# All sixteen modulation tiles of the even output projection moved into the opening stage, six per pair of weight tiles

## The reference, cut to what matters

```python
def adaln(cvec, w, b):
    mod = jax.nn.silu(cvec) @ w + b
    return jnp.split(mod, 6, axis=-1)          # shift1 scale1 gate1 shift2 scale2 gate2
...
    hs = modulate(rmsnorm(xs, norm1_g[l]), m_lat[0], m_lat[1])
...
    # layer 0: even_project, diff_attention, multiscale_pool, even_output (ends in "@ w_out")
    xs = xs + m_lat[2] * out_s
    hs = modulate(rmsnorm(xs, norm2_g[l]), m_lat[3], m_lat[4])
    xs = xs + m_lat[5] * swiglu(hs, w_ffn_in[l], w_ffn_out[l])
```

## Time and profile before

| | |
|---|---|
| median of 3 runs | 2965.31 us |
| the profiled execution, its own time | 2965.08 us |
| its span in the trace | 2962.3 us |
| PE busy | 2772.4 us (94%) |
| PE weight loads busy | 2646.7 us (89%) |
| DVE busy | 1310.1 us (44%) |
| ACT busy | 817.0 us (28%) |
| POOL busy | 765.0 us (26%) |
| `wmt` tiles of 512 KB by L191 | 56, 3.5 us from issue to landing |

### The profile page before, as it was taken

One profiled execution on the slowest core, in us unless ns is written; L12 is line 12 of the kernel. 1 busy time (PEld: TensorE's weight loads), 2 busy tenths in 40 slices (PEclk: granted clock), 3 DMA queues, 4 the chain that ended last, 5 costly groups with the idle time before them and its releaser, 6 DMA issues. The chain is left out here.

```text
span 2962.3 us, 40371 instructions
## 1 busy us (share of the span) xinstructions
PE 2772.4 (94%) x16562; PEld 2646.7 (89%) x16562; DVE 1310.1 (44%) x2125; ACT 817.0 (28%) x1277; POOL 765.0 (26%) x338
## 2 busy tenths in 40 slices
PE   5998888999999999999899996879999999999997
PEld 4997767989999999999899994549999999999996
DVE  5688985953222222222654444544422222222225
ACT  4214665251111111111532222542511111111113
POOL 1562223531111111111322212334321111111112
PEclk9998999999999999999999997999999999999999
DMA  6433102411111111110234434305111111111101
GB/s 241 165 130 87 22 15 107 157 58 43 43 42 42 42 42 42 42 42 18 108 121 148 150 113 187 111 24 217 43 58 43 42 42 42 42 38 38 40 13 64
DMA packets 57724, 227.13 MB, mean 77 GB/s; under 512 B 7376, under 2 KB 17296, under 8 KB 47120
## 3 DMA queue, kind: packets, MB, share of 16 engines
q1 hardware_dynamic: 56032, 225.12, 21.5%
q10 hardware_dynamic: 1584, 0.51, 0.1%
HBM read 191.52 MB, written 29.88 MB: 75 GB/s over the span
## 5 line engine op out<-in xcount | busy, mean ns | idle before, releaser
L220 PE MATMUL ps<-hh,wi_hi 128*128 128x384 f32 x2112 | 707.9, 335 | 0.0
L221 PE MATMUL ps<-hl,wi_hi 128*128 128x384 f32 x2112 | 705.8, 334 | 0.0
L222 PE MATMUL ps<-hh,wi_lo 128*128 128x384 f32 x2112 | 705.7, 334 | 0.0
L1166 DVE TENSOR_TENSOR hid<-ps,hid 128x384 f32<-128x384 f32 x132 | 73.6, 557 | 989.3 <-ACT hid L871 989.3
L220 PEld LDWEIGHTS ps<-hh,wi_hi 128*128 128x128 f32 x2112 | 396.7, 188 | 1.0 <-issue 0.3
L221 PEld LDWEIGHTS ps<-hl,wi_hi 128*128 128x128 f32 x2112 | 396.7, 188 | 1.0 <-issue 0.3
L222 PEld LDWEIGHTS ps<-hh,wi_lo 128*128 128x128 f32 x2112 | 396.7, 188 | 0.0
L871 ACT ACTIVATE hid<-ps 128x384 f32<-128x384 f32 x132 | 64.9, 492 | 1127.9 <-PE ps L222 1127.9
L998 POOL TENSOR_TENSOR wi_lo<-raw_in,wi_hi 128x2048 fp32r<-128x2048 f32 x44 | 202.9, 4611 | 645.4 <-ACT wi_hi L861 645.3
L1177 DVE SCALAR_TENSOR_TENSOR x<-ps,mod,x 128x128 f32<-128x128 f32 (+1 forms) x704 | 326.9, 512 | 77.0 <-PE ps L222 72.9
L220 PE MATMUL ps<-hid_hi,wo_hi 128*128 128x384 f32 x1056 | 354.0, 335 | 2.8 <-DVE x L1177 2.7
(11 more groups left out here) (268 smaller groups left out, 4542.9 us busy)
## 6 DMA issues: line engine op xcount, KB each, us to landing
raw_in<-in_w_ffn_in_dram SPq DMA_DIRECT2D x44, 1024.0 KB, 4.7
wmt<-in_w_mod_t_dram SPq DMA_DIRECT2D x56, 512.0 KB, 3.5
raw_out<-in_w_ffn_out_dram SPq DMA_DIRECT2D x22, 1024.0 KB, 4.7
gla_spill<-turn SPq DMA_DIRECT2D x24, 576.0 KB, 2.8
oraw<-in_w_in_odd_dram SPq DMA_DIRECT2D x24, 512.0 KB, 4.5
wmt_odd<-in_w_mod_t_dram SPq DMA_DIRECT2D x24, 512.0 KB, 5.6
x<-in_x_dram SPq DMA_DIRECT2D x8, 1152.0 KB, 11.0
wm<-in_w_mod_dram SPq DMA_DIRECT2D x16, 512.0 KB, 11.3
```

What stands on the lines that cost most here:

```text
L220: pe.matmul(acc, w_hi, in_hi, start=first, stop=False)
L221: pe.matmul(acc, w_hi, in_lo, start=False, stop=False)
L222: return pe.matmul(acc, w_lo, in_hi, start=False, stop=last)
L1166: dve.tensor_tensor(hid[:, t], ps[:, 2 * t + 1, 0:CW], hid[:, t], ALU.mult).then_inc(hid_done, 1)
```

## The change

In the diff, the lines from `ModulationBeside(... W0 + 14 * WB ...)` on are those of `trunk`, where `MODS` is 0 in layer 0 now. The opening computes 48 tiles beside its products instead of 32 (tiles 16 to 63), six per pair instead of four, and makes the scales of layer 0's second and of layer 1's first norm. `trunk(0, ...)` has no modulation tiles any more. On PE in the opening the mean stands ahead of the first modulation rows; groups 0 and 1 are made before the first product, and the rows of group g+2 stand between the products of channel tiles 2g and 2g+1, their columns behind both.

```diff
+        MODS = 6
...
-            mods = ModulationBeside(sem, k, ps, o, o + 16 * D, MOD_FIRST, 32, (1,))
+            mods = ModulationBeside(sem, k, ps, o, o + 16 * D, MOD_FIRST, MODS * PAIRS, (1, 2))
...
-                    for t in range(4):
-                        mods.load(sp, 4 * p + t)
+                    for t in range(MODS):
+                        mods.load(sp, MODS * p + t)
...
-                modulation_rows(0)
                 pe.wait_ge(cleared, 3)
                 pe.wait_ge(summed, KT)
                 for c in range(NC):
                     mm = pe.matmul(ps[:, c, 0:CW], ones[:], stat[:, cs[c]], start=True, stop=True)
                 mm.then_inc(averaged, 1)
-                modulation_columns(0)
+                for g in range(2):
+                    modulation_rows(g)
+                    modulation_columns(g)
                 for g in range(GROUPS):
-                    if g + 1 < GROUPS:
-                        modulation_rows(g + 1)
-                        modulation_columns(g + 1)
                     first_pair(2 * g)
+                    if g + 2 < GROUPS:
+                        modulation_rows(g + 2)
                     first_pair(2 * g + 1)
+                    if g + 2 < GROUPS:
+                        modulation_columns(g + 2)
...
-                    for t in range(4):
-                        mods.multiply(dve, 4 * p + t)
+                    for t in range(MODS):
+                        mods.multiply(dve, MODS * p + t)
                     if p in (3, 5):
                         rope((p - 3) // 2)
...
-            mods = ModulationBeside(sem, k, ps, W0 + 14 * WB, o + 4 * WB, first_mod, MODS, scales)
+            mods = ModulationBeside(sem, k, ps, W0 + 14 * WB, o + 4 * WB, first_mod, MODS) if MODS else None
...
-                mods.load_row(sp)
-                mods.load(sp, 0)
-                mods.load(sp, 1)
+                if mods is not None:
+                    mods.load_row(sp)
+                    mods.load(sp, 0)
+                    mods.load(sp, 1)
...
-                for m in range(min((MODS - 1 - 1) // 3 + 3, KT - 1) + 1, KT):
+                for m in range(max((MODS - 2) // 3 + 4, 4), KT):
                     weights.load(sp, m)
...
-                mods.silu(act)
+                if mods is not None:
+                    mods.silu(act)
...
-                mods.finish(dve)
```

More of the change, by code:

```diff
@@ L741, in ready, with trunk @@
             pe.wait_ge(self.o_low, c + 1)
-    def trunk(layer, weights, residual, in_hi, in_lo, first_mod, groups, scales=(), odd=None, result=None, pending=None):
+    def trunk(layer, weights, residual, in_hi, in_lo, first_mod=None, groups=0, odd=None, result=None, pending=None):
         s, sem, ps, k = stage()
@@ L2486, in build @@
     trunk(0, even_out, inp["x"], lambda kk, cols: (o_hi[kk] if kk < HEADS else p_hi[kk - HEADS])[:, cols],
-          lambda kk, cols: (o_lo[kk] if kk < HEADS else p_lo[kk - HEADS])[:, cols], 6 * KT, 4, (2,), odd=inp["w_in_odd"], pending=last_head)
+          lambda kk, cols: (o_lo[kk] if kk < HEADS else p_lo[kk - HEADS])[:, cols], odd=inp["w_in_odd"], pending=last_head)
     recycle()
```

## The result

| | before | after |
|---|---|---|
| median of the runs | 2964.87 us (4 runs, 2963.41 to 2969.42) | 2983.84 us (4 runs, 2982.59 to 2986.12) |
| profiled execution | 2965.08 us | 2986.12 us |
| its span, mean granted clock | 2962.3 us, 0.974 | 2984.0 us, 0.970 |
| DVE's last modulation sum of the opening | 251.10 | 283.32 |
| attention's first cast | 252.86 | 284.77 |

The ratio is 1.0062, with a 95% interval of 1.0045 to 1.008: slower by 19.0 us between the medians, where 17.7 were forecast. One execution of experiment 6 ran in the chip's slower state (4091.5 us, granted clock 0.631), and the median given there is that of its other five.

The account below looks back on a forecast made before the run. PE sets the opening's rhythm, but DVE ends with it, so DVE's work beyond its idle time lengthens the kernel. Opening +33.8, even output projection -16.1, sum +17.7 on 2965.08: forecast 2983 us, 8-in-10 range 2961 to 2996.

Parts of the forecast that it names:

- The opening's start: Opening: with the new PE order DVE reaches its modulation tiles 5.0 us earlier, at 70.5; bounds 3 and 7 us.
- The price of a tile: Opening: each modulation tile costs DVE the stage average of 3.93 us, so sixteen more cost 62.9 us.
- Full exclusion: Rival, opening: all POOL work in DVE's idle windows lands on DVE, 68.7 us for sixteen tiles, total 2988.6; chance 0.18.
- The waits: Opening: DVE's three long waits for modulation tiles, 27.6 us, disappear; the short ones grow from 6.9 to 10.4.
- Rotations: Opening: DVE's two rotations take 15.3 us, counted apart from the modulation tiles.
- the opening's +33.8: Opening: DVE ends at 284.9 instead of 251.1, 33.8 us later.
- The hidden cascade: Opening: late key rotation delays PE's last two weight tiles, start near 237, end near 262, hidden by DVE's tail.
- cascade: Rival, opening: POOL's work moves into DVE's tail, last twelve tiles cost 9.7 us more, total 2993 to 2996; chance 0.13.
- The trunk: Even output projection: without its sixteen tiles the second mean starts 16.1 us earlier; bounds 12.8 and 18.2.
- The clock at 1.00 through the projection: Even output projection: sign expected in the changed kernel's profile, granted clock at 1.00 throughout.
- the added products fit: Rival, opening: extra tiles run mostly in present waits at 2.72 us each, total 2958 to 2963; chance 0.12 under 2959.4.
- The sum: Whole kernel: +33.8 in the opening less 16.1 in the projection gives +17.7 us, forecast 2983 us.

Follow-up runs that it names:

- experiment 6: Changed kernel with, in both trunks, DVE's evictions (7, 1) and (6, 2) moved ahead of norm streams and ACT's square of (7, 1) ahead of its casts: 2981.69 us.
- Experiments 1: Unchanged kernel with only the new order on PE at the opening's start, 32 tiles there and 16 in the trunk: 2960.0 us, ratio 0.9979.
- experiments 2: Changed kernel with the old order on PE at the opening's start, all 48 tiles in the opening: 2988.68 us, ratio 1.0073.
- experiment 3: Changed kernel without POOL's pooling windows in the opening, weight splits kept: 2957.23 us, ratio 0.9966.
- experiment 9: New order on PE, forty tiles in the opening placed 6, 6, 6, 5, 5, 4, 4, 4 per pair instead of five each: 2956.48 us, ratio 0.9973.
- experiments 4: Changed kernel with forty tiles in the opening, five per pair, and eight in the even output projection, new order: 2955.94 us, ratio 0.9966.
- experiment 5: Unchanged kernel with the 16 modulation tiles of the even output projection computed nowhere, their columns holding only bias: 2953.47 us, ratio 0.9958.
- 10: Changed kernel with its 48 opening tiles placed 7, 7, 7, 7, 6, 5, 5, 4 per pair instead of six each: 2986.01 us, ratio 1.0072.
- experiment 7: New order on PE, 36 tiles in the opening (5, 5, 5, 4, 5, 4, 4, 4 per pair), 12 in the even output projection: 2954.98 us, ratio 0.9963.
- 8: New order, 36 tiles in the opening and 12 in the projection, plus evictions moved ahead of the norm: 2954.6 us, ratio 0.9962.

## Why the prediction was right, point by point

**The opening's start**: DVE at its tiles at 70.5 predicted, 70.58 found. Experiments 1 (69.72) and 2 (75.34) show that the order makes it. Undone in the changed kernel it costs 6.9 us in the trace, the 4.8 of the later start and more waits for loads; done alone it gains 6.2.

**The price of a tile**: 3.93 us predicted; found 283.32 - 70.58 = 212.7 us, less 20.2 of waits, less the rotations (172.37 to 180.97 and 233.14 to 236.67, 12.1 us), 180.4 for 48 tiles, 3.76 each. 0.17 x 48 = 8.2 us less than forecast. Taking the average over the stage, and not the undisturbed 2.72, was the choice that decided the sign, and experiment 3 shows POOL's instructions to be the reason. Full exclusion, 68.7 us for sixteen tiles, was the wrong end.

**The waits**: this step was wrong. The 27.6 us of long waits were counted as gone and the short ones as 10.4 together. Found were 20.2 us in 17 pieces, the longest 4.7: the three long ones went, but three others of 2.5, 2.6 and 4.7 us stand in their place, behind SP's queue of raw weights and turning DMAs, and fourteen of under 2 us. That is 9.8 us more than forecast. Rotations were 3.2 less (12.1 against 15.3). Together: 0.1 for the start, and -8.2 - 3.2 + 9.8 = -1.6, 283.3 where 284.9 was forecast (the rest is rounding). So the opening's +33.8 came as +32.2 at DVE's end and +31.9 at attention by errors that nearly cancel, and that was luck: no step of the prediction tied them to each other. In the runs they do move against each other: in experiment 3 the price fell from 3.76 to 3.03 us and the waits rose by 9.3, in experiment 9 the waits fell by 2.4 and DVE ended no earlier.

**The hidden cascade**: PE's last two tiles were to start near 237 and end near 262. They started at 241.5 and ended near 269, behind waits for splits of 6.71 and 6.24 us, hidden by DVE's tail of 14.84 us. As forecast, the stall cost nothing, and the rival "cascade" did not become a price.

**The trunk**: 16.1 us to the second mean predicted, 15.7 found, by the chain that was named, with two small errors in it: the first mean came 1.4 us earlier than forecast, but from its end to the norm DVE needed 4.3 us and not 2.5. Then follow 12.0 us from DVE's norm (625.01) to the end of POOL's addition (637.02), as before to the tenth. The term that was missing is the clock's. "The clock at 1.00 through the projection" held from 613.0 to the first mean (0.98 from 529.7 to 613.0), but the 4.01 us wait that this chain leaves at its end is followed by slow matmuls that cost 2.9 us. In before that wait was 0.52 us. The same wait of 4.0 us stands in experiments 2 to 5, 9 and 10, and the price behind it is not fixed: 2.8 to 2.9 us in 2, 9 and 10 as in after, 1.4 in 3, 4 and 5. In experiment 6, without the wait, the stretch is gone too, and in 7, with 1.36 us, nothing is lost. What decides between 1.4 and 2.9 is open.

**The rivals**: "the added products fit" fell, as attention began at 284.8 and not before 274; that the windows were the reason is experiment 3. "Full exclusion" (2988.6) lies 4.8 us above the result, "cascade" 9. The versions between, experiments 4 and 7, are where a gain was to be had: up to 36 tiles the opening is still PE's. Attention begins at 246.62, 248.50, 257.32 and 284.77 with 32, 36, 40 and 48 tiles: 0.5 us for each of the first four, 2.2 for each of the next four, 3.4 for each of the last eight. What the trunk gives is read from the traces, from PE's first product of the projection to ACT's take-out behind the slow stretch (656.09 in before, 158.0 us): 148.8 us with twelve tiles left (experiment 7), 144.6 with eight (4), 145.1 with none (after) and 144.5 in experiment 5. So 9.2 us for the first four that leave it, 13.4 for the first eight, and 12.8 to 13.5 for all sixteen: nothing for the last eight.

**The sum** came within 1.3 us (19.0 against 17.7). The opening was 1.9 us better than forecast, attention 0.3 shorter, the trunk 0.4 worse, and the clock's 2.9 had been left out. The mechanism was right; that the number is so near is in part luck.

**The best version** found is 36 to 40 tiles with the new order: 2955 to 2956 us, 0.34 to 0.38% below before and about 0.95% below the change; experiments 4, 7 and 8 are not to be told apart. By the stages of the traces 36 should be some 4.6 us better than 40; the medians don't show it, and attention's changing length stands between. In the seam it stays open why POOL's addition gets in ahead of DVE when it starts 0.7 us behind the norm's first instruction (experiment 6) and waits for the stream's end when it starts in its middle.

## What to carry to other kernels

Price work that is to be moved beside other work by the average of the stage it goes to, with its neighbours on the shared port, not by its undisturbed duration. And put the marginal piece, not the whole, on the scale: here the receiving stage takes 4 tiles for 2 us, 8 for 11 and 16 for 38, while the giving stage pays 9, 13 and 13. When a wait is expected to stay or to grow, look up what PE's clock did after the last such wait, and add it as a range. Before a trace is compared with another, look at a stage that neither kernel changes: its difference is the scatter.

## What the hardware showed beyond that

- A POOL addition of 1.01 us (128x384) takes 5.48 to 5.50 us when it starts within DVE's stream of norm instructions (before, after, experiments 1 to 5, 7, 9 and 10), and ends 0.9 us after the stream. Where PE waits 4.0 us for it, its granted clock then averages 0.73 over 10 us in after and experiments 2 and 10, 0.74 in 9, and 0.89 in 3, 4 and 5.
- The pooling windows are 85 us of POOL's time and cost DVE 30.2 us on its 96 instructions beside them: about a third of POOL's time is paid again by the other engine.
- Taking a wait for PE away in the SwiGLU's start brought three shorter ones for DVE (3.1 us): of the 4.01 us wait and the slow stretch behind it, 2.4 us were gained in the trace and 2.2 in the medians.
